# Constant products in TensorE's waits, and f32r-split latent projections, in a two-block transformer kernel

## The reference, cut to what matters

```python
def _mla_mixer(u, positions, w_down, q_norm, kv_norm, w_uq, w_ukv, w_out):
    cq, ckv, k_rope = jnp.split(u @ w_down, [384, 640], axis=-1)          # "mlad"
    q = (_rmsnorm(cq, q_norm) @ w_uq)                                      # "mlaq": 384 -> 8 x 192
    kv = (_rmsnorm(ckv, kv_norm) @ w_ukv)                                  # "mlak", "mlav": 256 -> 8 x 256
    ...rope on q_rope and k_rope, softmax attention of 8 heads, then @ w_out

def diff_attention(...):
    s = einsum('bhcqd,bhckd->bhcqk', qi, kt)       # two maps c of each of 4 heads
    p = softmax(where(mask, s, NEG_BIG))
    a = p[:, :, 0] - lam * p[:, :, 1]
    return einsum('bhqk,bhkv->bhqv', a, v)
```

## Time and profile before

| | |
|---|---|
| median of 3 executions | 3549.57 us |
| lowest and highest | 3542.15 and 3553.04 us |
| the profiled execution's own time | 3553.95 us |
| its span, first to last instruction | 3552.2 us |
| TensorE busy | 3448.3 us (97%) |
| VectorE, ScalarE, GpSimd busy | 42%, 28%, 42% |
| mean granted TensorE clock | 0.976 of 2.4 GHz |
| HBM read | 356.41 MB, 101 GB/s over the span |

### The profile page before, as it was taken

The page is one execution under the profiler, slowest core; times in us unless marked ns, Lnnn a source line. Parts: engine busy times, 40 slices in busy tenths (PEclk is TensorE's granted clock), DMA queues, the critical chain, the costliest instruction groups (busy, mean ns, idle before and its releaser), DMA issues.

```text
span 3552.2 us, 41450 instructions
## 1 busy us (share of the span) xinstructions
PE 3448.3 (97%) x16504; PEld 2746.7 (77%) x16504; DVE 1478.7 (42%) x2571; ACT 1009.6 (28%) x1256; POOL 1500.0 (42%) x505
## 2 busy tenths in 40 slices
PE   7999999899999999999999999989999999899999
PEld 6878777578887888765788886867888868678887
DVE  6565267855253524135411126854101168542010
ACT  2222322622223222303322233434212234342121
POOL 3545452035455545510254554502546545125463
PEclk9999999999999999999999999989999999899999
DMA  6544222025352434211123222201222222012222
GB/s 260 191 147 191 93 83 72 1 84 201 124 202 100 189 136 159 89 43 66 60 87 108 88 96 71 84 25 48 92 98 95 95 71 84 24 37 94 95 95 82
DMA packets 54874, 360.65 MB, mean 102 GB/s; under 512 B 6080, under 2 KB 6464, under 8 KB 17728
## 3 DMA queue, kind: packets, MB, share of 16 engines
q1 hardware_dynamic: 54720, 358.53, 28.0%
HBM read 356.41 MB, written 2.10 MB: 101 GB/s over the span
## 4 chain that ended last, share of the span: by engine, by line
PE 91%; DVE 5%; ACT 2%; issue 1%; DMA 1%; POOL 0%; SPq 0%; DVEq 0%; ACTq 0%; POOLq 0%
PE LP L533 82%; PE XB L533 8%; ACT E L1282 1%; PE LP L891 1%; DMA big<-w_ada 1%; DVE wk L2053 0%; POOL w_lo L1778 0%; PE XB L775 0%; DVE XB L1979 0%; ACT sq L1282 0%; DVE gain L2121 0%; PE XB L737 0%; DVE big L2163 0%; ACT Z L1282 0%; DVE big L2162 0%
## 5 line engine op out<-in xcount | busy, mean ns | idle before, releaser
L1778 POOL TENSOR_TENSOR w_lo<-ring,w_hi 128x2048 fp32r<-128x2048 f32 (+1 forms) x263 | 1125.8, 4281 | 774.7 <-ACT w_hi L1282 774.5
L533 PE MATMUL LP<-u_hi,w_hi 128*128 128x512 f32 x2480 | 979.0, 395 | 17.3 <-ACT u_hi L1282 14.0
L533 PE MATMUL LP<-u_hi,w_lo 128*128 128x512 f32 x2480 | 972.8, 392 | 0.0
L533 PE MATMUL LP<-u_lo,w_hi 128*128 128x512 f32 x2480 | 942.7, 390 | 0.0
L533 PE MATMUL LP<-big_r,w_hi 128*128 128x512 f32 x2432 | 751.1, 390 | 4.0 <-POOL w_lo L1778 3.3
L1282 ACT ACTIVATE w_hi<-ring 128x2048 fp32r<-128x2048 f32 (+1 forms) x263 | 468.5, 1781 | 860.5 <-PE LP L533 704.4
L533 PEld LDWEIGHTS LP<-u_hi,w_hi 128*128 128x128 f32 x2480 | 470.7, 190 | 134.0 <-issue 34.6
L533 PE MATMUL LP<-big_r,w_lo 128*128 128x512 f32 x1472 | 573.4, 390 | 0.0
L533 PEld LDWEIGHTS LP<-u_hi,w_lo 128*128 128x128 f32 x2480 | 470.6, 190 | 99.0
L533 PEld LDWEIGHTS LP<-u_lo,w_hi 128*128 128x128 f32 x2480 | 466.5, 188 | 95.8 <-issue 0.5
L533 PEld LDWEIGHTS LP<-big_r,w_hi 128*128 128x128 f32 x2432 | 456.5, 188 | 100.0 <-issue 3.4
(11 more groups left out here) (321 smaller groups left out, 3481.5 us busy)
## 6 DMA issues: line engine op xcount, KB each, us to landing
ada_in<-w_ada SPq DMA_DIRECT2D x66, 1024.0 KB, 4.9
ring<-w_in SPq DMA_DIRECT2D x22, 1024.0 KB, 4.8
ring<-w_gu00a SPq DMA_DIRECT2D x11, 1024.0 KB, 7.0
ring<-w_gu00b SPq DMA_DIRECT2D x11, 1024.0 KB, 6.6
ring<-w_gu01a SPq DMA_DIRECT2D x11, 1024.0 KB, 6.7
ring<-w_gu01b SPq DMA_DIRECT2D x11, 1024.0 KB, 6.7
ring<-w_gu10a SPq DMA_DIRECT2D x11, 1024.0 KB, 6.7
ring<-w_gu10b SPq DMA_DIRECT2D x11, 1024.0 KB, 7.0
```

What stands on the lines that cost most here:

```text
L533: return pe.matmul(o, lhsT=lhsT, rhs=rhs, start=start, stop=stop)
L1778: gp.tensor_tensor(w_lo[:, slab % RING, 0:width], ring[:, slab % RING, 0:width], w_high(q, width).bitcast(F32), ALU.subtract).then_inc(s(" ...
```

## The change

1. TensorE gets filling products that nothing reads: `fill(n)` multiplies the constant identity by 256 columns of a constant mask into a PSUM bank that is free at that point. In `total_sum` two stand behind the first sums and two behind the last, in `spread` four behind the spreading products, for the five norms that `norm` makes itself. In `diff_attention` 2 to 5 stand at nine of the units, ahead of `beside(n)`, 29 in each of the two layers, and 4 ahead of it.
2. mlaq, mlak and mlav are cut as the other layers are: ScalarE rounds the five latent chunks and 14 more slabs, GpSimd subtracts them, and a product is three f32r passes.
3. The attention behind mlav waits for the PSUM pairs only ahead of the first product by the values, no longer ahead of the first scores. `turn` of the key's rope comes one slab later, the queries' ropes behind keys 0 and 2, and their tiles move from S to wk.

```diff
+        kv_high = over("kv_high", [P, 2, T], "wk", 4)
...
-        ORDER += [("mlad", 3, DC * 256, 0, 1), ("mlaq", 6, 3 * 256, 0, 0), ("mlak", 4, 2 * 256, 0, 0),
-                  ("mlav", 4, 2 * 256, 0, 0), ("mlao", 4, DC * 256, 0, 1)]
+        ORDER += [("mlad", 3, DC * 256, 0, 1), ("mlaq", 6, 3 * 256, 0, 1), ("mlak", 4, 2 * 256, 0, 1),
+                  ("mlav", 4, 2 * 256, 0, 1), ("mlao", 4, DC * 256, 0, 1)]
...
+            def fill(n, bank=XB[3]):
+
+                for _ in range(n):
+                    mm(bank[:, 0:256], cc("ident"), cc("causal", 0, 256))
+
+            def fill_heads(n, times):
+
+                if times and pl.head + n // NB > 1:
+                    pe.wait_ge(s("o_taken"), pl.head + n // NB - 1)
+                fill(times, LP[0][:, (pl.head + n // NB) % 2, :])
+
-            def total_sum(late=0):
+            def total_sum(late=0, filled=0):
...
+                fill(min(filled, 2))
                 if pl.wo:
...
                 pl.wo = False
-
-            def spread(late=0):
+                fill(min(filled, 2))
+
+            def spread(late=0, filled=0):
...
                 last.then_inc(s("rstd_spread"), 1)
+                fill(filled)
...
-                    total_sum()
-                    spread()
+                    total_sum(filled=4)
+                    spread(filled=4)
...
+                    fill_heads(n, {0: 5, 2: 5, 6: 2, 8: 2, 9: 3, 11: 2, 13: 3, 16: 5, 18: 2}.get(n, 0))
                     beside(n)
...
-                pl.groups_taken()
-                if pl.rope:
-                    pe.wait_ge(s("rope_done"), pl.rope)
+                pe.wait_ge(s("rope_done"), pl.rope)
...
+                        if i == 0:
+                            pl.groups_taken()
                         pe.wait_ge(s("pt_done"), k + 1)
...
+            def latent(c):
+                if c not in latents_cut:
+                    latents_cut.add(c)
+                    pl.got("latent_cut")
+                return latent_high(c), big_r[:, c, :]
...
-            linear("mlaq", "fm", lambda c: big[:, CQ + c, :], after=behind_queries)
+            linear("mlaq", "fm", lambda c: latent(CQ + c), after=behind_queries)
...
+                slab_taken(13)
+                fill(4, LP[(first + 13) % 2][:, 0, :])
                 pe.wait_ge(s("level_taken"), 16 * (l + 1))
                 pl.groups_taken()
                 diff_attention(l, diff_score, lambda hh, b: av[:, b, blk(hh)], beside_maps)
...
+            def round_latents(k):
+
+                act.wait_ge(s(f"lin_taken{(first + k) % 2}"), (first + k) // 2 + 1)
+                for c in ((0, 1), (2, 3), (4,))[k]:
+                    f(latent_high(c), big[:, c, :], ACT.Copy).then_inc(s("latent_high"), 1)
+
+            def latent_roots(k, it):
+                if k < 2:
+                    pl.got("latent_summed")
+                    f(latent_root(k), XB[3][:, 4 * k:4 * k + NB], ACT.Sqrt, scale=1.0 / (384, 256)[k], bias=cc("eps"))\
+                        .then_inc(s("latent_root"), 1)
+                if k == 0:
+                    round_latents(2)
+
+            layer("mlad", latent_square, behind=lambda k: round_latents(k) if k < 2 else None)
+            layer("mlaq", latent_roots)
+            layer("mlak")
+            layer("mlav", last=True)
...
+            def latent_rests(k):
+                for c in ((0, 1), (2, 3), (4,))[k]:
+                    pl.got("latent_high")
+                    gp.tensor_tensor(big_r[:, c, :], big[:, c, :], latent_high(c).bitcast(F32), ALU.subtract)\
+                        .then_inc(s("latent_cut"), 1)
...
+            def query_turns(k):
+                if k % 2 == 0:
+                    turn((QR + k, QR + k + 1), tabs[:, 3, :], wk[:, 2:4, :])
+
+            layer("mlad", behind=latent_rests)
+            layer("mlaq", behind=key_turn)
+            layer("mlak", behind=query_turns)
+            layer("mlav", last=True)
```

More of the change, by code:

```diff
@@ L301, in latent_root, with latent_high @@
             return st[:, 16 + 4 * i + b:16 + 4 * i + b + n]
+        def latent_high(c):
+            return big_r[:, KN + c, :] if c < CKV else kv_high[:, c - CKV, :]
         def latent_squares(c):
@@ L975, in behind_keys @@
             def behind_keys(k):
-                if k < 2:
-                    slab_taken(3 + 4 + k)
-                    rotate((QR + 2 * k, QR + 2 * k + 1), cc("rot64"))
+                if k % 2 == 0:
+                    slab_taken(3 + 4 + k // 2)
+                    rotate((QR + k, QR + k + 1), cc("rot64"))
+            latents_cut = set()
+            def latent(c):
[3 more added lines that the diff above has]
+                return latent_high(c), big_r[:, c, :]
             linear("mlad", "fm", src, fresh=fresh, after=lambda k: latent_sums(0, range(CQ, CQ + 3)) if k == 2 else None)
             slab_taken(1)
-            linear("mlaq", "fm", lambda c: big[:, CQ + c, :], after=behind_queries)
-            linear("mlak", "fm", lambda c: big[:, CKV + c, :], after=behind_keys)
-            linear("mlav", "tm", lambda c: big[:, CKV + c, :])
+            linear("mlaq", "fm", lambda c: latent(CQ + c), after=behind_queries)
+            linear("mlak", "fm", lambda c: latent(CKV + c), after=behind_keys)
+            linear("mlav", "tm", lambda c: latent(CKV + c))
             def mla_score(hh, qb, bank):
@@ L1409, in hrms @@
                 pl.norm += 1
[L1411 to L1415, removed]
             def ffn(l, j, up, down, per=1):
@@ L1801, in layer @@
                 pl.cut += n
-            def skip(*names):
-                pl.group += sum(WIDTH[x_][0] for x_ in names)
             def low_hidden(n, per):
@@ L1919, in _, with key_turn @@
             first_input()
-            layer("mlad", last=True)
-            skip("mlaq", "mlak", "mlav")
-            turn([KR] + list(range(QR, QR + 4)), tabs[:, 3, :])
+            def latent_rests(k):
[3 more added lines that the diff above has]
+                        .then_inc(s("latent_cut"), 1)
+            def key_turn(k):
+                if k == 2:
+                    turn((KR,), tabs[:, 3, :], wk[:, 2:4, :])
+            def query_turns(k):
+                if k % 2 == 0:
+                    turn((QR + k, QR + k + 1), tabs[:, 3, :], wk[:, 2:4, :])
[3 more added lines that the diff above has]
+            layer("mlav", last=True)
             layer("mlao", last=True)
@@ L2546, in queries_taken @@
                     latent_recip(1)
-                if k == 1:
-                    turn((KR,), tabs[:, 2, :])
+                if k == 2:
+                    turn((KR,), tabs[:, 2, :], wk, wk[:, 2:4, :])
                 if k == 2:
@@ L2553, in keys_taken @@
                 keys(k, it, p)
-                if k < 2:
-                    turn((QR + 2 * k, QR + 2 * k + 1), tabs[:, 2, :])
+                if k % 2 == 0:
+                    turn((QR + k, QR + k + 1), tabs[:, 2, :], wk, wk[:, 2:4, :])
             def values_taken(k, it, p):
```

## The result

| | before | after |
|---|---|---|
| median | 3548.86 us (4 runs, 3542.15 to 3553.04) | 3509.48 us (4 runs, 3506.33 to 3515.98) |
| ratio to before | | 0.9891, 95% interval 0.9873 to 0.9909 |
| the profiled execution's own time | 3553.95 us | 3506.33 us |
| TensorE busy, mean granted clock | 97%, 0.976 | 98%, 0.993 |
| VectorE, ScalarE, GpSimd busy | 42%, 28%, 42% | 42%, 29%, 44% |

The account below looks back on a forecast made before the run. TensorE was taken to bound the kernel nearly throughout. The terms -15.8 (norms), -11.2 (split), -1.0 (attention behind mlav) and -11 (two-map attentions) sum to -39.0, forecast 3510 us after allowing for the profiled execution standing 4.4 above the median; range 3496 to 3534.

Parts of the forecast that it names:

- The norms: In five norms, fills keep TensorE's clock up: -15.8 us, bounds -16.1 and +9.5.
- the rate of 0.36 us: Cost of each us at 1.2 GHz, read in mlad's norm; 44.4 us of all five norms cost 16.1.
- the 0.3 for fills past their waits: In the five norms together, 0.3 us charged for fills that outlast TensorE's waits.
- The split: In mlaq, mlak and mlav, products take three passes: -9.2 and -2.0, sum -11.2 us, the added work hidden.
- The starved split: Rival: TensorE waits for `w_lo` ahead of the 14 slabs, the split turns to +2.8, 3525 us; chance 0.06.
- The attention behind mlav: First scores no longer wait for VectorE to take the last pair: -1.0 us, between 0 and -1.3.
- the rival, -6.6 more: Rival: the latent attention's start runs at the higher clock too, -6.6 us more, 3504; chance 0.16.
- The two-map attentions: In both layers' two-map attentions, fills raise the clock: -11 us, between -15.9 and 0.
- the chosen 0.32: Chosen average cost of each us at 1.2 GHz in the two-map attentions; 50.5 us give 15.9.
- the fives: Five fills at unit 0 of each two-map attention without a wait to fill in full: 2.0 us taken off the gain.
- the places without a fill: In the two-map attentions, unit 4 and the sum behind the maps stay slow: 2.8 us taken off the gain.
- The slower rival: Rival: fills don't hold the clock; norms +9.5, maps +15.2 a layer, in all +27.7, 3577 us; chance 0.04.

Follow-up runs that it names:

- e3: The kernel before plus only the split with its new order of turns, no fills and the wait for the PSUM pairs where it was: 3541.02 us, ratio 0.9977.
- e10: The changed kernel with the second queries' turn behind key slab 3, without the five fills at unit 0 of each two-map attention: 3507.23 us.
- e9: The kernel before plus only the eight fills of the norm ahead of hyb: 3545.86 us, ratio 0.9989.
- e6: The changed kernel with each fill cut from 256 columns to 1: 3544.90 us, ratio 0.9981.
- e7: The changed kernel with VectorE's part of the second queries' turn behind the taking of key slab 3 in place of 2: 3509.95 us.

## Why the prediction was right

The forecast, 3510 us, stands 0.5 from the median. Its sum of -39.0 was made against the profiled execution, and that pair of executions differs by 47.6. So the mechanisms were right, and that the number came so near is partly luck. Term by term:

- **The norms**, -15.8: 11.1 in the changed kernel's trace, 11.2 to 14.3 in the seven others with these fills. Hyb, gu10 and mlad were forecast at 2.5 each and gave 2.4, 2.3 and 2.3, so the rate of 0.36 us for each at the lower clock held, and the 0.3 for fills past their waits as well. The step that failed is that the fills hold the clock in gu01 and gu11 too. There 16 records of one column run on end, and the clock fell under or behind them: in gu01 in all eight traces with these fills (c3 or c7 remain), in gu11 in four. Where it didn't, gu11 gave 3.7, the forecast's 3.8; from c7 to c0 that is 3.1 us for 6.8, 0.46 for each.
- **The split**, -11.2: 10.1 at equal clock (e3). The price of a pass was right: with the late turn the stage gives 11.4. The missing 1.1 to 1.3 us are a wait of TensorE, and the prediction had named its place, "VectorE's part of a turn waits for GpSimd's, and behind it stand the latent copies and takings", but costed it at nothing. The starved split did not come: there is no wait for `w_lo`. By the isolated gap of 216 ns that the Trainium skill gives in "TensorE: Matmul & The Clock Gate", section "Back-to-back issue gap", the estimate had been 12.9; the passes are 0.227 us apart here, and the stage agrees with that.
- **The attention behind mlav**, -1.0: 1.6 for the wait, beyond the bound of 1.3; nothing of it came back. The half-clock stretch was taken to stay and the rival, -6.6 more at a chance of 0.16, came true with -7.3. The experiments say that the moved wait did it. The prediction listed this as the rival's reason and didn't trust it.
- **The two-map attentions**, -11: -12.1 in the trace and 1.7 behind, 13.3 alone by time. (0.32 x 50.5 is 16.2 and not the 15.9 of the sum, which hides 0.3.) With the 3.3 that the first fives cost (e10) it is 15.4 for 50.5 us at 1.2 GHz, 0.30 for each; the chosen 0.32 holds. Off it came 2.0 for the fives, which was too little, and 2.8 for the places without a fill, which was too much: the clock held at unit 4 although its wait of 2.5 us stayed.
- **Not in the sum**: the paired attention's 4.9 us. Nothing in the prediction looked at this attention.

So in this pair of traces two gains that it had not counted (4.9 and 7.3) outweigh the 4.7 missing in the norms; the 1.1 of the split doesn't show in this pair, since only the trace of before has 3.4 us at 1.2 GHz there. Over many executions the first of them counts for less (e9), and the executions of before that give the median are on average faster than the profiled one. The number was hit more closely than its terms. The slower rival fell: the fills with 256 columns held the clock in three norms and both attentions. Its mechanism exists, and e6 shows it: had the fills been thin, there had been nothing for it but cost. (Its +9.5 for the norms is 9.1 by its own terms, 3.5 - 1.69 = 1.8 five times.)

## What to carry to other kernels

Where TensorE bounds a kernel, read the granted clock by stage and price a us at the lower clock by equal work at both levels: 0.3 to 0.5 us here, and 0.2 where another engine bounds much of the stretch. Fill waits with wide products of constants that end with the wait, and look at narrow products as you look at waits, for TensorE can be busy and still lose its clock. A change of 1 us in a stage is shown by the same instruction's start in two traces, not by a median that scatters by 10.

## What was not expected of the hardware

- **The scatter of this kernel goes mostly with its clock.** Of the 17 executions of before beside e9 the shortest (3542.84 us) had a mean clock of 0.980 and the longest (3556.05) 0.976. The 0.004 are 28 us more at 1.2 GHz, for 13.2 us of time (the clock is given to 0.001, which is 7 us at 1.2 GHz). A line through all 17 gives 0.36 us for each; the three other groups of before give 0.44, 0.32 and, with seven executions, 0.26. Which stretches fall in one execution and not in the next isn't seen, as each kernel has one trace; the traces of different kernels do differ in stretches that none of the edits touches.
- **The clock fell while TensorE was busy with narrow products.** In the trace of before TensorE waits 0.4 us in all in the paired attention's first 20 us, of which 17 are at 1.2 GHz; in after the clock falls under gu11's 16 sums of one column; and with e6's thin fills TensorE is busy for 10.20 us of 11.00 at a clock of 0.69. That the narrowness is the cause is argued from these, and only e6 varied it.
- **A VectorE add with both inputs in SBUF stands still while a GpSimd instruction runs that started before it.** L2312 takes 0.69 us alone. It took 1.69 beside GpSimd's products and 1.37 beside its subtraction, and in all these cases ended 0.55 us after GpSimd's instruction did, however much of that was left. It costs far more where GpSimd's instruction is long: six of the adds `wk<-wk,sq` of L2099 in the trace of after began beside a 2048-wide subtraction and took 4.33 us on average, against 0.69 for the four that didn't, and L2099 holds 1% of the chain that ended last. The products of L2310, which read one input from PSUM, took 0.68 beside GpSimd's work as well as alone. And who comes first isn't held: in e7 an add of 0.69 was on when a subtraction began, and it was the subtraction that took 1.45 in place of 1.29. What it is in the machine that they share, these runs don't show. Two of the six adds of after with GpSimd's two subtractions (which end at 748.25, the second add at 748.80), and the subtraction of e7:

```profile
739.94 8.86 DVE L2099 TENSOR_TENSOR wk<-wk,sq 128x512 f32<-128x512 f32 x2 [0.70 <-ACT sq L1312]
738.61 9.64 POOL L1812 TENSOR_TENSOR w_lo<-ring,w_hi 128x2048 fp32r<-128x2048 f32 x2 [5.07 <-ACT w_hi L1312]
...
1580.11 1.45 POOL L1812 TENSOR_TENSOR w_lo<-ring,w_hi 128x512 fp32r<-128x512 f32 x1 [1.58 <-ACT w_hi L1312]
```
